# RWKV block inverse: from 64x64 tiles over six levels to 32x32 tiles over five, with the transpose kept beside it

## What is computed

```python
def wkv7_scan(r, w, k, v, a, bb, reverse):
    ...
    def step(state, inp):
        r_t, w_t, k_t, v_t, a_t, b_t = inp
        sa = jnp.einsum('bhvk,bhk->bhv', state, a_t)
        state = state * w_t[:, :, None, :] + sa[..., None] * b_t[:, :, None, :] + v_t[..., None] * k_t[:, :, None, :]
        y = jnp.einsum('bhvk,bhk->bhv', state, r_t)
        return state, y
    s0 = jnp.zeros((b, nh, n, n), F32)
    _, y = lax.scan(step, s0, seq, reverse=reverse)
```

## Time and profile before

| | |
|---|---|
| median of 3 runs | 1380.3 us (lowest 1379.02) |
| the profiled execution | 1379.52 us, its span 1377.5 us |
| TensorE's granted clock over the span | 0.995 |
| TensorE busy | 1328.0 us, 96% |
| VectorE busy | 869.5 us, 63% |
| ScalarE busy | 354.0 us, 26% |
| the core, from its first product (924.95) to `ty1` (1110.47) | 185.5 us |

### The profile page before, as it was taken

One profiled execution on the slowest core, in us unless ns is written; L12 is line 12 of the kernel. 1 busy time (PEld: TensorE's weight loads), 2 busy tenths in 40 slices (PEclk: granted clock), 3 DMA queues, 4 the chain that ended last, 5 costly groups with the idle time before them and its releaser, 6 DMA issues. The chain is left out here.

```text
span 1377.5 us, 24975 instructions
## 1 busy us (share of the span) xinstructions
PE 1328.0 (96%) x10772; PEld 1012.3 (73%) x10772; DVE 869.5 (63%) x1455; ACT 354.0 (26%) x755; POOL 119.6 (9%) x184
## 2 busy tenths in 40 slices
PE   7999999999999998899999999998999999999999
PEld 6868548689995444469998467847778765999943
DVE  4577612567778347538898567458444364798973
ACT  2311200312221014412332013703432331233300
POOL 5745000000000001010000000031000000000000
PEclk9999999999999999999999999999999999999999
DMA  8433224335444724045444543400011042454452
GB/s 303 173 129 134 104 91 153 130 138 184 175 145 171 249 73 166 0 153 184 175 145 171 206 160 123 184 1 3 4 33 34 27 160 91 154 183 147 161 183 92
DMA packets 16733, 182.30 MB, mean 132 GB/s; under 512 B 1648, under 2 KB 3952, under 8 KB 6000
## 3 DMA queue, kind: packets, MB, share of 16 engines
q1 hardware_dynamic: 14320, 175.12, 35.0%
q10 hardware_dynamic: 2304, 5.59, 1.1%
HBM read 179.65 MB, written 1.05 MB: 131 GB/s over the span
## 5 line engine op out<-in xcount | busy, mean ns | idle before, releaser
L1697 PE MATMUL banks<-xn,arena 128*128 128x128 f32 x1440 | 165.7, 275 | 0.0
L1697 PEld LDWEIGHTS banks<-xn,arena 128*128 128x128 f32 x1440 | 163.2, 192 | 0.0
L1714 PE MATMUL banks<-arena 128*128 128x512 f32 x264 | 122.0, 592 | 0.0
L1697 PE MATMUL banks<-hT,weight_ring 128*128 128x128 f32 x960 | 116.5, 275 | 0.0
L1697 PEld LDWEIGHTS banks<-hT,weight_ring 128*128 128x128 f32 x960 | 111.8, 192 | 0.0
L1423 PE MATMUL banks<-weight_ring,arena 128*128 128x512 f32 x224 | 98.7, 597 | 0.8 <-ACT arena L1313 0.8
L1714 PEld LDWEIGHTS banks<-arena 128*128 128x128 f32 x264 | 49.8, 190 | 60.7 <-issue 60.7
L1714 PE MATMUL banks<-weight_ring,arena 128*128 128x512 f32 x198 | 93.3, 592 | 0.0
L2642 DVE SCALAR_TENSOR_TENSOR arena<-arena,prm 128x255 f32<-128x255 f32 x200 | 87.4, 479 | 5.4 <-ACT arena L1068 3.6
L1423 PEld LDWEIGHTS banks<-weight_ring,arena 128*128 128x128 f32 x224 | 42.8, 193 | 51.9 <-issue 50.3
L3060 DVE COPY_PREDICATED weight_ring<-masks,banks 128x512 f32<-128x512 uint8 x48 | 35.1, 734 | 66.7 <-PE banks L2004 60.2
(11 more groups left out here) (443 smaller groups left out, 2204.7 us busy)
## 6 DMA issues: line engine op xcount, KB each, us to landing
weight_ring<-in_wall SPq DMA_DIRECT2D x81, 2048.0 KB, 8.2
weight_ring<-in_wall SPq DMA_DIRECT2D x2, 1024.0 KB, 7.2
x<-in_x_tok ACTq DMA_DIRECT2D x2, 512.0 KB, 4.6
arena<-in_mem_tok SPq DMA_DIRECT2D x1, 1024.0 KB, 17.4
arena<-in_wall SPq DMA_DIRECT2D x1, 1024.0 KB, 5.0
arena<-in_wide SPq DMA_DIRECT2D x2, 512.0 KB, 4.5
out_y<-x ACTq DMA_DIRECT2D x4, 256.0 KB, 2.0
arena<-in_masks ACTq DMA_DIRECT2D x1, 896.0 KB, 9.4
```

The source lines that it names most:

```text
L1697: ins = mm(b_(n)[:, j * P:(j + 1) * P], lhsT=weights[:, kb, j * P:(j + 1) * P], rhs=features_[:, kb, :], start=opens and j == 0 and kb == ...
L1714: ins = mm(b_(n), lhsT=a, rhs=b, start=pair == 0, stop=pair == FB // 2 - 1)
```

## The change

The inverse of a 64-block is now put together from its two diagonal blocks of 32 and one corner of 32. The levels 0 to 4 (blocks of 1 to 16) run on 32x32 tiles of the array, four at once on its diagonal, tile (32r, 32r) for the four 32-blocks of a 128-token tile. T and its transpose are both kept (`T32`, second index a = 0 or 1), and each level computes both, so nothing is turned in a level: `first_products` gives Y, `closing_products` gives the new T and, with the operands swapped, its transpose. The corners of 64 take the place of level 5: `across_products` makes L T for the corner, `turned_diagonal` writes the turned diagonal blocks (a product with the identity, groups `tf`) and `turned_corners` the corner, already turned (groups `to`). `inverse_out` puts both into `Tf`. T32 has two buffers, one for odd and one for even steps. The order between the pieces is written anew: the key products for the values (`products(j, 1, ...)`) move behind their step, beside the next one; the gate and `ty1` move behind step 3's inverse. All results of a 32x32 group for the four row positions go to one PSUM bank, in four separate quarters of its partitions. Before, the two row positions of `four_tiles` wrote to two banks of a pair.

```diff
-LEVELS = 6
+LEVELS = 5
+QUARTER = [slice(32 * r, 32 * r + 32) for r in range(4)]
...
+def core_groups(j):
+    last = j + 1 == len(STEPS)
+    later = (j, 1) if last else (j + 1, 0)
+    out = level_groups("tl", j, 0)
+    if j:
+        out += key_products(j - 1, 1, 2)
...
+    out += level_groups("yl", j, 4) + key_products(*later, 0) + level_groups("tl", j, 4) + key_products(*later, 1)
+    out += level_groups("yl", j, 5) + key_products(*later, 2) + [(f"tf{j}{h}", 1, "pair") for h in HALVES]
+    out += key_products(*later, 3) + [(f"to{j}{h}", 1, "pair") for h in HALVES]
...
@@ buffers
-        Tc = [ap.rearrange("p (k b c) -> p b k c", k=4, b=2) for ap in T_rows]
-        Tt, Yb = [[quads(half_of(ap, h)) for h in HALVES] for ap in (lent[:, 2, 0, 1024:2048], lent[:, 2, 1, 0:1024])]
+        T32 = [lent[:, 2, 0, 1024 * i:1024 * i + 1024].rearrange("p (a k c) -> p a k c", a=2, c=32) for i in range(2)]
+        Yb = lent[:, 2, 1, 0:512].rearrange("p (k c) -> p k c", c=32)
...
@@ ScalarE
+            def first_out(j, lv):
+                for h in HALVES:
+                    n = G[f"yl{j}{lv}{h}"]
+                    act.wait_ge(psum_full, n + 1)
+                    A(Yb[:, 8 * h:8 * h + 8, :], narrow_(n)[:, 0], ACT.Copy).then_inc(bank_sem(n), 1)
+            def inverse_out(j):
+                d = STEPS[j][0]
+                for h in HALVES:
+                    evict_pair(Tf[h], G[f"tf{j}{h}"])
+                for h in HALVES:
...
+                    for r in (d, 2 + d):
+                        ins = A(Tf[h][QUARTER[r], :, :, QUARTER[1 - d]], corners_(n)[QUARTER[r]], ACT.Copy)
...
@@ TensorE
+            def level_zero(j):
...
+                    for k in range(8):
+                        for a in range(2):
+                            for r in range(4):
+                                at = QUARTER[r]
+                                sides = (L[at, k, 0, time_of(k, r)], ident[at, at])
+                                ins = mm(narrow_(n)[at, a, k], lhsT=sides[a], rhs=sides[1 - a], start=True, stop=True,
+                                         tile_position=(32 * r, 32 * r))
+            def first_products(j, lv):
...
+                    for k in range(8):
+                        for r in range(4):
+                            at = QUARTER[r]
+                            ins = mm(narrow_(n)[at, 0, k], lhsT=L[at, k, 0, time_of(k, r)], rhs=T_[at, 0, 8 * h + k],
+                                     start=True, stop=True, tile_position=(32 * r, 32 * r))
+            def closing_products(j, lv):
...
+                    for k in range(8):
+                        for a in range(2):
+                            for r in range(4):
+                                at = QUARTER[r]
+                                sides = (T_[at, 1, 8 * h + k], Yb[at, 8 * h + k])
+                                ins = mm(narrow_(n)[at, a, k], lhsT=sides[a], rhs=sides[1 - a], start=True, stop=True,
+                                         tile_position=(32 * r, 32 * r))
+            def across_products(j):
...
+                    for k in range(8):
+                        for side in range(2):
+                            first, second = 2 * side + d, 2 * side + 1 - d
+                            ins = mm(narrow_(n)[QUARTER[second], 0, k], lhsT=L[QUARTER[first], k, 0, time_of(k, second)],
+                                     rhs=T_[QUARTER[first], 0, 8 * h + k], start=True, stop=True,
+                                     tile_position=(32 * first, 32 * second))
+            def turned_diagonal(j):
...
+                                ins = mm(quads_(n)[QUARTER[to], swap, k], lhsT=T_[QUARTER[r], 0, 8 * h + 4 * swap + k],
+                                         rhs=ident[QUARTER[r], SIDE[r // 2]], start=True, stop=True,
+                                         tile_position=(32 * r, 32 * to))
+            def turned_corners(j):
...
+                                ins = mm(corners_(n)[QUARTER[to], swap, k], lhsT=Yb[QUARTER[second], head],
+                                         rhs=T_[QUARTER[second], 1, head], start=True, stop=True,
+                                         tile_position=(32 * second, 32 * to))
...
-                    pe.wait_ge(*when_read(G[f"tf{j}{h}"]))
+                    pe.wait_ge(*when_read(G[f"to{j}{h}"]))
...
+                if j in (1, 2):
+                    products(j, 1, 0)
+                    products(j, 1, 1)
                     for h in HALVES:
+                        s_out(j - 1, h)
+            for tt in (1, 0):
+                gate(tt)
+            y_tokens(1)
...
@@ VectorE
-                mask = masks[:, m0:m0 + HD].unsqueeze(1).unsqueeze(1).to_broadcast([P, 2, 4, HD])
+                mask = masks[:, m0:m0 + HD].rearrange("p (a c) -> p a c", a=2).unsqueeze(2).to_broadcast([P, 2, 8, 32])
...
-                    V.copy_predicated(Tc[h], mask, quads_(n)).then_inc(bank_sem(n), 1)
+                    V.copy_predicated(T32[j % 2][:, :, 8 * h:8 * h + 8, :], mask, narrow_(n)).then_inc(bank_sem(n), 1)
...
@@ GpSimd
-            for j in range(1, len(STEPS)):
-                for h in HALVES:
-                    pool.wait_ge(psum_full, G[f"tf{j - 1}{h}"] + 1)
-                    g.tensor_copy(Tc[h], unit).then_inc(t_identity, 1)
+            for j in range(2, len(STEPS)):
+                pool.wait_ge(psum_full, G[f"to{j - 2}1"] + 1)
+                g.tensor_copy(T32[j % 2], unit).then_inc(t_identity, 1)
```

More of the change, by code:

```diff
@@ new lines, in _ @@
+                first_products(j, 2)
+                for h in HALVES if j else ():
+                    block_solve(j - 1, h, "u1")
+                if j == 0:
+                    products(0, 1, 1)
+                closing_products(j, 2)
+                for h in HALVES if j else ():
+                    x_finish(j - 1, h)
+                if j == 0:
+                    pe.wait_ge(*when_read(G["bonus"]))
+                    transposes(G["tx_bonus"], [bonus_rows[:, tt * P:(tt + 1) * P] for tt in range(TT)])
@@ new lines, in _ @@
+                first_products(j, 3)
+                for h in HALVES if j else ():
+                    block_solve(j - 1, h, "u2")
+                closing_products(j, 3)
+                for h in HALVES if j else ():
+                    y_out(j - 1, h)
+                first_products(j, 4)
+                products(*later, 0)
+                closing_products(j, 4)
+                products(*later, 1)
+                across_products(j)
+                products(*later, 2)
+                turned_diagonal(j)
@@ L3122, in _ @@
             dve.wait_ge(lent_zero, 2)
[L3123 to L3125 removed]
+            for i in range(4):
+                products(0, 0, i)
             n = G["bonus"]
@@ new lines, in _ @@
+                later = (j + 1, 0) if j + 1 < len(STEPS) else (j, 1)
+                level(j, 0)
+                if j:
+                    products(j - 1, 1, 2)
+                    products(j - 1, 1, 3)
+                else:
+                    second_direction(0)
+                    dve.wait_ge(lent_zero, 4)
+                    products(0, 1, 0)
+                level(j, 1)
+                if j == 0:
+                    second_direction(1)
+                    products(0, 1, 1)
+                level(j, 2)
@@ new lines, in _ @@
+                for h in HALVES if j else ():
+                    y_sum(j - 1, h)
+                products(*later, 0)
+                level(j, 4)
+                products(*later, 1)
+                if j == 0:
+                    second_direction(4)
+                products(*later, 2)
+                products(*later, 3)
+                if j == 1:
+                    dve.wait_ge(kept_zero, 4)
+                if j in (1, 2):
+                    products(j, 1, 0)
+                    products(j, 1, 1)
+                    for h in HALVES:
+                        s_scale(j - 1, h)
```

326 lines of the change are left out of this document (148 added, 178 removed).

## The result

The changed kernel takes 1514.4 us (median of 4 runs, 1511.7 to 1515.5) against 1379.7 for the kernel before: a ratio of 1.098, 95% interval 1.0956 to 1.1004. The forecast was 1371, its range 1360 to 1420. The profiled execution has a span of 1513.3 us.

The account below looks back on a forecast made before the run. The prediction took TensorE, busy 1328.0 of 1377.5 us, to bound the kernel. From 1379.5 us it took off 9.6 for less matmul work and added 1.5 for new waits: 1371 us, range 1360 to 1420.

Parts of the forecast that it names:

- The pace of a small matmul: In the inverse's levels, a round of 32x32 matmuls with 32 columns was put at 0.032 us, between bounds 0.027 and 0.059.
- rival 3: In the inverse's small matmuls, a round doesn't shrink and stays at 0.059 us; kernel at 1419 us, chance 0.07.
- The line through 128 and 64 columns: Round time for small matmuls was extended from 0.112 us at 128 columns, 0.053 less at 64, to 0.032 at 32.
- rival 4: In the 32x32 groups, four row positions take turns at their common PSUM bank; kernel at about 1565 us, chance 0.06.
- What goes and where: On TensorE up to `ty1`, 89.8 us of the old inverse go and 80.2 us of small matmuls come.
- what stands behind the core: From `ty1` to `ty0`, 23.2 us end on VectorE's chain, so nothing is won there.
- The step on new waits: In the core, TensorE's waits outside the levels become 9.2 to 9.5 us from 7.9, losing 1.5 us.
- rival 2: In the levels, TensorE waits for instruction fetch, 5 us a step; kernel at 1391 us, chance 0.10.
- rival 5: In the core's levels, 32x32 rounds on four of sixteen tiles lower the clock to 1.2 GHz; 1424 us and up, chance 0.09.

Follow-up runs that it names:

- the run by itself: The kernel before with 1024 small matmuls (2048 records, 32x32 tiles, 32 columns) put ahead of level 0 of step 0; 1437.0 us, ratio 1.042.
- the one-pass kernel: The changed kernel with first and closing products reading the upper 16 bits of operands as bfloat16, one pass instead of two; 1422.9 us, ratio 1.033.

## Why the prediction was wrong

**The pace of a small matmul** was right: 0.032 us a round of four forecast, 0.03 measured; rival 3 (0.059) falls. The line through 128 and 64 columns did not bend.

**The turns at a common bank** (rival 4): none. Four row positions write their quarters of one bank within the same 0.03 us. The Trainium skill, TensorEngine Tiling (Array Packing), Gotcha 1: PSUM Pressure, has different row tiles on different banks; by that the round would have been 0.13. The trace does not bear it out for tiles that write different partitions. The Trainium skill, TensorE: Matmul & The Clock Gate (Wait — 56ns, not 53.3ns?), gives a floor of about 25 ns from start to start. It doesn't hold over all tiles: 16 records in 0.12 us are 8 ns each; for one tile, 30 ns apart, it could.

**What goes and where**: what stands behind the core was right. VectorE's level copy costs 0.73 as taken, and behind `ty1` TensorE waits 3.2 us for VectorE as forecast (nearly 4). The step on new waits (9.2 to 9.5 us against 7.9, a loss of 1.5) can't be tested in the changed kernel, where the pauses hide them. The new order with the old inverse has 0.3 us more of idle time, and 2.8 less of busy time, a gain that the prediction didn't have.

**The failed step is rival 2, instruction fetch.** Its mechanism was right, down to 40 packets more and 128 records a block. Its size was not: I let a block arrive "as fast as one packet and one more such time", 2 us, so a level with 3 blocks would take 6, and took 5 us a step after catching up, 20 us in all, at a chance of 0.10. Measured by itself, a block comes every 3.5 to 4.0 us, 1.8 to 2.1 of it a pause after the 128th record, and in the changed kernel the pauses grew by 62.9 us. A level of 384 records thus takes 10 to 12 us where it was to take 3; the three pieces or so that stand in it use few instructions, but don't save that. The packet's own 1.0 us says how long it travels, not how often one comes: in the run by itself a packet began 1.0 to 1.7 us into a burst and the next burst 2.2 to 3.0 us later, so that these two add up, and not two packet times. What I should have set beside it stood in the earlier trace rows: a level of before uses its 136 records in 3.90 us, one block in 3.7. Its whole trace has no 128 records in less than 3.54 us, and no two q8 packets closer than 3.30. So "128 records in 1.0 us" asked for 3.5 times the highest rate that the trace had ever shown, of a supply whose limit it didn't show. That bound, one block in 3.7 us, gives 9234 / 128 x 3.7 = 267 us for the core, not 177, if nothing else binds: some 1460. It should have been the likeliest case, or at least the end of the range.

The Trainium skill, Runtime: NRT & Kernel Launch, Instruction fetch mechanics, has 2048 instructions held and the fetch mostly hidden. In the run by itself the first burst, after a stretch of few instructions, had 208 records, 416 instructions; then each block was waited for. I let the page lower the chance, with a trace that had no stretch to test it.

**The clock** (rival 5) fell, but not for the reason given. "The 32x32 rounds keep four of sixteen tiles busy" is refuted by the 512-column run on those tiles, 1.00. It fell with long pauses in the kernel before and with bursts of short records on tiles of both sizes. Its size was off too: 62 us were put on the rounds alone, and with the pieces between them at 0.50 as well for most of the core it came to about 78.

The two are worked out apart only by sum (62.9 of pauses, 71.5 of more busy time), since no run has pauses like those of the changed kernel at the full clock. Open is why the kernel with 64-column records kept a clock of 0.88 and the one-pass kernel 0.67 at nearly the same pauses (36 and 40 us); no run took that apart, and the times of both spread over 12 us from one execution to the next.

## What to carry to other kernels

Before splitting work into smaller matmuls, count instructions: records in the densest stretch that the trace shows, per us, are the rate that is known to be supplied; what goes beyond it must be measured, for example with a run of such matmuls put into the kernel as it is. On this chip 128 fp32 records need 3.5 to 4 us, 27 ns or more each, so splitting pays only while a record takes longer than that on average. Here fewer passes gave what smaller tiles did not. And a stretch in which TensorE pauses for long costs again in the work between the pauses, at half the clock.

## What was not expected of the hardware

A block of TensorE's instructions is followed by a pause of 1.8 to 2.1 us even where hardly anything else happens on the core, so the fetch of the next is not hidden behind the 1.5 to 1.9 us in which one is used. The clock stayed at 0.50 for 26 us in which TensorE was busy for 25.1, most of them with records of 32 columns on 64x64 tiles. And four row positions of the array share a bank at 8 ns a record.
